# A hybrid retention / differential-attention step: the first attention tiles between the last products of the value projection

## The reference, cut to what matters

```
v_d = h @ w_in[:, 5120:6144]                    # values, 640 tokens x 8 heads of 128
s   = einsum('bqhmd,bkhmd->bhmqk', q, k) * 64**-0.5    # two maps (m = 0, 1) of each head
p   = softmax(s);  a = p[:, :, 0] - lam * p[:, :, 1]
o   = einsum('bhqk,bkhe->bqhe', a, v)
branch_d = (rmsnorm(o) * (1 - lam_init)) @ w_diff_out
```

## Time and profile before

| | |
|---|---|
| median of 3 runs | 1314.18 us (1314.15 to 1314.39) |
| the profiled execution | 1314.83 us, of it the span of the trace 1313.2 us |
| PE busy | 1263.9 us (96%) |
| DVE, ACT, POOL busy | 798.2, 487.5, 307.6 us |
| attention: first scores to last output | 625.25 to 743.6 us |
| a 1 MB weight load | lands a median 5.5 us after its issue |

### The profile page before, as it was taken

The page is one execution under the profiler, slowest core; times in us unless marked ns, Lnnn a source line. Parts: engine busy times, 40 slices in busy tenths (PEclk is TensorE's granted clock), DMA queues, the critical chain, the costliest instruction groups (busy, mean ns, idle before and its releaser), DMA issues.

```text
span 1313.2 us, 19818 instructions
## 1 busy us (share of the span) xinstructions
PE 1263.9 (96%) x7734; PEld 1155.6 (88%) x7734; DVE 798.2 (61%) x1292; ACT 487.5 (37%) x812; POOL 307.6 (23%) x269
## 2 busy tenths in 40 slices
PE   4999999999999999999799899999999999999997
PEld 2698887799999999988688799889998999989986
DVE  4654121466657733463799754378984689547966
ACT  5452223344331112222777532245441244313434
POOL 1011000311000111120699700003520355005500
PEclk9999999999999999999899999999999999999999
DMA  9634222144444434362000034220233122322222
GB/s 307 206 97 136 64 74 71 41 148 141 127 131 130 142 104 127 106 192 97 33 1 1 10 121 153 88 64 27 71 119 106 33 81 89 120 64 64 89 89 80
DMA packets 87392, 129.56 MB, mean 99 GB/s; under 512 B 3529, under 2 KB 64450, under 8 KB 87186
## 3 DMA queue, kind: packets, MB, share of 16 engines
q1 hardware_dynamic: 76880, 95.17, 22.7%
q0 software_dynamic: 9104, 32.20, 8.0%
q10 hardware_dynamic: 1330, 1.10, 0.3%
HBM read 117.43 MB, written 4.73 MB: 93 GB/s over the span
## 4 chain that ended last, share of the span: by engine, by line
PE 85%; POOL 6%; DVE 4%; ACT 3%; issue 1%; DMA 1%; SPq 0%; ACTq 0%; DVEq 0%
PE psum L421 31%; PE psum L458 28%; PE psum L664 17%; POOL probs L961 4%; POOL probs L967 3%; PE psum L1024 1%; PE psum L407 1%; DMA ada_a<-in_w_ada 1%; PE psum L594 1%; PE psum L522 1%; DVE w_lo L390 1%; PE psum L1132 1%; PE psum L1130 1%; PE psum L1131 0%; ACT probs L1531 0%
## 5 line engine op out<-in xcount | busy, mean ns | idle before, releaser
L390 DVE TENSOR_TENSOR w_lo<-w_raw,w_hi 128x2048 fp32r<-128x2048 f32 x57 | 130.6, 2291 | 200.9 <-ACT w_hi L385 197.6
L385 ACT ACTIVATE w_hi<-w_raw 128x2048 fp32r<-128x2048 f32 x57 | 108.8, 1909 | 173.7 <-PE psum L458 107.5
L421 PE MATMUL psum<-h_hi,w_lo 128*128 128x320 f32 x672 | 154.7, 311 | 0.8 <-ACT y_nat L1474 0.8
L421 PE MATMUL psum<-h_hi,w_hi 128*128 128x320 f32 x672 | 153.1, 309 | 0.0
L421 PE MATMUL psum<-h_lo,w_hi 128*128 128x320 f32 x672 | 153.0, 309 | 0.0
L458 PE MATMUL psum<-w_hi,hid 128*128 128x512 f32 x440 | 135.5, 389 | 0.0
L421 PEld LDWEIGHTS psum<-h_hi,w_lo 128*128 128x128 f32 x672 | 111.8, 188 | 1.7 <-issue 1.7
L421 PEld LDWEIGHTS psum<-h_lo,w_hi 128*128 128x128 f32 x672 | 112.3, 188 | 0.0
L421 PEld LDWEIGHTS psum<-h_hi,w_hi 128*128 128x128 f32 x672 | 112.3, 188 | 0.0
L664 PE MATMUL psum<-h_hi,seven_lo 128*128 128x320 f32 x320 | 98.9, 309 | 1.1 <-DVE silu_g L2189 1.1
L664 PE MATMUL psum<-h_lo,seven_hi 128*128 128x320 f32 x320 | 98.9, 309 | 0.0
(11 more groups left out here) (302 smaller groups left out, 2771.7 us busy)
## 6 DMA issues: line engine op xcount, KB each, us to landing
w_raw<-in_w_in SPq DMA_DIRECT2D x32, 1024.0 KB, 5.5
ada_b<-in_w_ada POOLq DMA_DIRECT2D x32, 512.0 KB, 4.0
w_raw<-in_w_ffn_gate SPq DMA_DIRECT2D x11, 1024.0 KB, 5.4
w_raw<-in_w_ffn_up SPq DMA_DIRECT2D x11, 1024.0 KB, 5.4
ada_a<-in_w_ada SPq DMA_DIRECT2D x8, 1024.0 KB, 13.3
w_raw<-in_w_ffn_down SPq DMA_DIRECT2D x8, 1024.0 KB, 5.1
w_raw<-in_w_ret_out SPq DMA_DIRECT2D x4, 1024.0 KB, 5.2
swapped<-qk_d POOLq DMA_DIRECT2D x32, 128.0 KB, 2.6
```

The source lines that it names most:

```text
L385: act.activation(w_hi[s][:, :, :], w_raw[s][:, :, :], ACT.Copy).then_inc(w_hi_done, 1)
L390: dve.tensor_tensor(w_lo[s][:, :, :], w_raw[s][:, :, :], w_hi[s][:, :, :].bitcast(F32), ALU.subtract).then_inc(w_lo_done, 1)
L421: last = pe.matmul(bank(4 * par + 2 * j + h, HALF), w[:, k, cs], x[:, k, h * HALF:(h + 1) * HALF], start=(k == 0 and n == 0), stop=(k == K ...
```

## The change

- The last (i, par) = (1, 1) of `v_d` takes its tiles in the order 0, 2, 1, 3, 4. `scores(0)` stands ahead of it, `scores(1)` behind its third tile, `scores(2)` behind its fourth. The eight matmuls of L407 for both par stand together ahead of `scores(0)`.
- ACT interleaves: both copies of the sums, the table for Exp, `exp(0)`, three tiles of `v_d`, `exp(1)`, a tile, `exp(2)`, a tile. `scores(1)` waits until ACT has copied three tiles of the group.
- The weights of tiles 0 to 2 go to a new buffer `first_probs`, which lies where `w_raw` lies; so SP loads `diff_out`'s weights only after tile 2 has been transposed.
- The split of `diff_out`'s first unit moves into the attention: on ACT four pieces of 128x512 at the end of slots 8 to 11, on DVE eight pieces of 128x256 at the end of slots 14 to 21, each of which reads two tensors of SBUF.
- The prompt keys are transposed (PE) in slot 35 and copied (ACT) there; POOL stores them behind its last tile; DVE waits for that store ahead of `diff_out`'s results. SP stores `new_diff_v`.

The diff, cut to its core:

```diff
+ACT_SPLIT_SLOTS, DVE_SPLIT_SLOTS = range(8, 12), range(14, 22)
...
-        k_out = at("k_out", H + 16, [P, D])
+        k_out = at("k_out", H + 25, [P, D])
         probs = at("probs", H + 20, [P, 3, 2, TOK])
+        first_probs = at("first_probs", W, [P, 3, 2, TOK])
         mix_hi = at("mix_hi", H, [P, KT, TOK], F32R)
...
+        def weights_of(n, m):
+            return (first_probs if n < 3 else probs)[:, n % 3, m, :]
...
+        def act_split_part(act, unit, s, part, parts):
+            ks = slice(part * KT // parts, (part + 1) * KT // parts)
+            if part == 0:
+                act.wait_ge(w_landed[s], (unit - s) * 8 + 16)
+                act.wait_ge(mm_done, unit * 2 - 2 + AHEAD)
+            done = act.activation(w_hi[s][:, ks, :], w_raw[s][:, ks, :], ACT.Copy)
+            if part == parts - 1:
+                done.then_inc(w_hi_done, 1)
+        def dve_split_part(dve, unit, s, part, parts):
+            ks = slice(part * KT // parts, (part + 1) * KT // parts)
+            if part == 0:
+                dve.wait_ge(w_hi_done, unit + 1)
+            done = dve.tensor_tensor(w_lo[s][:, ks, :], w_raw[s][:, ks, :], w_hi[s][:, ks, :].bitcast(F32), ALU.subtract)
+            if part == parts - 1:
+                done.then_inc(w_lo_done, 1)
...
-                        for t in range(TILES):
...
+                            if between and (i, par) == (1, 1):
+                                between(t)
+                    if between and i == 1:
+                        if par == 0:
+                            pe.wait_ge(freed[r], START[name][r] + TILES)
+                            pe.wait_ge(ada_step, 16 * (ADA_FIRST[name] + 3) + 32)
+                            for slot in range(2):
+                                last = sums_over_partitions(pe, slot, bank(1, 4, 4 * slot))
+                            last.then_inc(mm_done, 2)
+                            between(None)
+                        else:
+                            last.then_inc(mm_done, 2)
+                        continue
                     if name in ADA_FIRST:
                         if i == 1 and par == 0:
...
+            sp.dma_start(o["new_diff_v"][0, 0].rearrange("p h e -> p (h e)"), v_d[:, LAT_TILES, :]).then_inc(vd_stored, 16)
+            sp.wait_ge(at_T, 3)
             stream("diff_out", columns(by_tile["w_diff_out"], 0))
             stream_wide("w_o", by_tile["w_o"], 0)
...
-            pool.wait_ge(freed["act"], START["diff_out"]["act"])
-            pool.dma_start(o["new_diff_v"][0, 0].rearrange("p h e -> p (h e)"), v_d[:, LAT_TILES, :]).then_inc(vd_stored, 16)
-            pool.wait_ge(k_copied, 1)
-            pool.dma_start(o["new_diff_k"][0, 0].rearrange("p h m d -> p (h m d)"), k_out[:, :]).then_inc(k_stored, 16)
...
+            pool.wait_ge(k_copied, 1)
...
             pe_dense(pe, "k_d", pe_T_unit, h_hi, h_lo)
-            pe_wide(pe, "v_d", h_hi, h_lo)
-            pe.wait_ge(freed["act"], START["diff_out"]["act"])
             pe.wait_ge(rope_done, 12 + AHEAD)
-            for h in range(DH):
-                last = pe.transpose(bank(6 + h // 4, P, (h % 4) * P), qk_d[:, DH + h, LAT:TOK], ident[:, :])
-            last.then_inc(k_ps, 1)
-            pe.wait_ge(ld_vc, 16)
...
                 b0 = 3 * (n % 2)
                 if n >= 2:
                     pe.wait_ge(at_e, 2 * n - 2)
+                if n == 1:
+                    pe.wait_ge(freed["act"], START["v_d"]["act"] + TILES + 3)
...
             def weights_T(n):
                 full = is_long(n)
+                if n == 0:
+                    pe.wait_ge(freed["act"], START["v_d"]["act"] + TILES + 4)
...
             def outputs(n):
+                if n == 0:
+                    pe.wait_ge(freed["act"], START["diff_out"]["act"])
+                if n == GROUPS:
+                    pe.wait_ge(ld_vc, 16)
                 pe.wait_ge(at_aT, n + 1)
...
-            pe.wait_ge(k_copied, 1)
-            for slot in range(-1, QT + 4):
+            def prompt_keys_T():
+                pe.wait_ge(at_e, 2 * (QT - 1))
+                for h in range(DH):
+                    last = pe.transpose(bank(2 * (h // 4), P, (h % 4) * P), qk_d[:, DH + h, LAT:TOK], ident[:, :])
+                last.then_inc(k_ps, 1)
+            def early_scores(t):
+                if t in (None, 1, 3):
+                    scores((None, 1, 3).index(t))
+            pe_wide(pe, "v_d", h_hi, h_lo, between=early_scores)
+            for slot in range(2, QT + 4):
                 if 0 <= slot - 3 < QT:
                     weights_T(slot - 3)
+                if slot == QT + 1:
+                    prompt_keys_T()
                 if 0 <= slot - 4:
...
                 if slot + 1 < QT:
                     scores(slot + 1)
+            pe.wait_ge(k_copied, 1)
...
             dense("k_d", copy_T("k_d", qk_d, DH, 1.0))
-            dense_wide("v_d", copy_N("v_d", v_d, ACT.Copy, after=12))
-            act.wait_ge(r_ctx_out, RH * 32)
-            act.wait_ge(k_ps, 1)
-            act.activation(k_out[:, :], psum[:, 6 * BANK:8 * BANK], ACT.Copy).then_inc(k_copied, 1)
...
+            def keys_out():
+                act.wait_ge(k_ps, 1)
+                both = psum[:, 0:4 * BANK].rearrange("p (b c) -> p b c", b=2)[:, :, 0:BANK]
+                act.activation(k_out[:, :].rearrange("p (b c) -> p b c", b=2), both, ACT.Copy).then_inc(k_copied, 1)
...
+            act_split(act, unit_of("v_d", 1, 1), 1)
+            act.wait_ge(mm_done, 2 * unit_of("v_d", 1, 0) + 2 + AHEAD)
+            for par in range(2):
+                copy_ada("v_d", 1, par, bank(1, 4, 4 * par)).then_inc(ada_copied, 1)
             set_table(ACT.Exp)
-            for slot in range(QT + 3):
-                if slot >= 3:
-                    evacuate_T(slot - 3)
+            act.wait_ge(w_lo_done, unit_of("v_d", 1, 1) + 1)
+            exp(0)
+            v_d_tiles(1, (0, 2, 1))
+            exp(1)
+            v_d_tiles(1, (3,))
+            exp(2)
+            v_d_tiles(1, (4,))
+            for slot in range(3, QT + 3):
+                evacuate_T(slot - 3)
                 if slot < QT:
                     exp(slot)
+                if slot in ACT_SPLIT_SLOTS:
+                    act_split_part(act, unit_of("diff_out", 0, 0), 0, slot - ACT_SPLIT_SLOTS.start, len(ACT_SPLIT_SLOTS))
                 if slot == QT:
                     set_table(ACT.Sqrt)
+                if slot == QT + 1:
+                    keys_out()
             root("normo", DH * TILES)
             act.wait_ge(gate_T_ps, 1)
...
             dense("k_d", rotate("k_d", qk_d, 8, DH, 4, 128 + 256))
...
             dense_wide("v_d", nothing)
-            dve.wait_ge(freed["act"], START["diff_out"]["act"])
...
+            def late_modulation():
+                dve.wait_ge(ada_copied, 4)
...
+            late_modulation()
...
+                if slot in DVE_SPLIT_SLOTS:
+                    dve_split_part(dve, unit_of("diff_out", 0, 0), 0, slot - DVE_SPLIT_SLOTS.start, len(DVE_SPLIT_SLOTS))
...

```

More of the change, by code:

```diff
@@ L71 @@
 WIDE_BANKS = ((0, 1, 2, 6, 7), (3, 4, 5, 6, 7))
+LAST_TILES = (0, 2, 1, 3, 4)
 def wide_ready(name, i, t):
-    return (2 * WIDE.index(name) + i) * LAT_TILES + t + 1
+    place = LAST_TILES.index(t) if (name, i) == ("v_d", 1) else t
+    return (2 * WIDE.index(name) + i) * LAT_TILES + place + 1
 def lay_out_phases():
@@ L438, in wide, with pe_wide @@
             return w[:, 2 * k:2 * k + 2, :].rearrange("p a b -> p (a b)")
-        def pe_wide(pe, name, hi, lo, kt=KT, split=None):
+        def pe_wide(pe, name, hi, lo, kt=KT, split=None, between=None):
             r, half = READER[name][0], kt // 2
@@ L472, in pe_wide @@
                     else:
-                        for t in range(TILES):
+                        for t in LAST_TILES if between and (i, par) == (1, 1) else range(TILES):
                             if par == 0:
@@ L957, in _ @@
                 first = DVE_KEYS if is_long(n) else 0
-                p0, p1 = probs[:, n % 3, 0, first:size], probs[:, n % 3, 1, first:size]
+                p0, p1 = weights_of(n, 0)[:, first:size], weights_of(n, 1)[:, first:size]
                 pool.wait_ge(at_f, n + 1)
@@ L967, in _ @@
                 pool.tensor_tensor(p0, p0, p1, ALU.add).then_inc(at_a, 1)
+            pool.wait_ge(k_copied, 1)
+            pool.dma_start(o["new_diff_k"][0, 0].rearrange("p h m d -> p (h m d)"), k_out[:, :]).then_inc(k_stored, 16)
             pool.wait_ge(od_rstd, 1)
@@ L1434, in copy_N, with evacuate @@
             def copy_N(name, dst, func, after=0):
-                def evacuate(i):
+                def evacuate(i, tiles=range(TILES)):
                     if after:
                         act.wait_ge(rope_done, after + AHEAD)
-                    for t in range(TILES):
+                    for t in tiles:
                         wait_tile(act, name, i, t)
-                        if name in ADA_FIRST and t == LAT_TILES:
+                        if name in ADA_FIRST and t == LAT_TILES and i == 0:
```

(20 more changed lines are left out.)

14 lines of the change are left out of this document (7 added, 7 removed).

## The result

| | before | after |
|---|---|---|
| median | 1314.29 us (1314.15 to 1315.90, 4 runs) | 1323.62 us (1322.88 to 1324.84, 4 runs) |
| profiled execution, span | 1313.2 us | 1321.2 us |

The ratio is 1.0072, 95% interval 1.0059 to 1.0084: the change makes the kernel 9.3 us **slower**, where 2.1 us faster was forecast, and it lies outside the range of 1307.0 to 1315.0. The cause is one wait of TensorE, 9.1 us long, that the prediction overlooked. It begins some 45 us ahead of the point (606.80) from which the prediction's sum was made.

A forecast was written before the change was run, and what follows sets the result against it. It took four engines within 20% of one attention period, with PE setting the start: -8.0 from the earlier start, +5.8 from DVE's pieces, +0.1 at the end, ACT 0, sum -2.1, median 1312.1 us; range 1307.0 to 1315.0.

The forecast's parts named there:

- The start, by the new order: From the end of `v_d`'s third group (606.80), PE's steps sum to 23.2 us; POOL's first long tile comes 8.0 us earlier.
- Rival 4: Attention's start: POOL's first long tile stays at 638, ACT being the new bound; +5.9, 1320.1 us; chance 0.04.
- the ramp from there to the fifth long tile: Between POOL's first and fifth long tiles: two waits from DVE's evacuation of prompt tiles stay, so the gain remains 8.0 us.
- PE's wait ahead of `scores(1)`: Late in `v_d`, PE waits for ACT's copy of the third tile: 0.23 to start, 0.60 to run, 0.05; 0.88 us.
- ACT's four pieces, slots 8 to 11: In the attention, 0.60 us each in ACT's 0.53 of idle time: taken as 0, at most 0.3 us.
- a piece on DVE: Behind a maximum in slots 14 to 21, it waits for POOL's L967: a slot takes 3.82 us instead of 3.10, +0.72.
- eight pieces: DVE's split in attention slots 14 to 21: eight times +0.72, +5.8 us, with ends of +1.2 and +11.4.
- end of the attention: Eight prompt-key transposes in PE's slot 35, where PE waits for POOL anyway: +0.1 us; stores and weight loads 0.
- Nothing is caught up later: After the slots with DVE's pieces, the time lost stays lost, since PE needs its 3.10 us a slot.
- Rival 1: Slots 14 to 21: pieces slip past POOL and DVE alone pays 1.2 us; -6.7 in all, 1307.5; chance 0.14.
- Rival 2: Slots 14 to 21: a piece begins only behind L967's end plus a hand-over, 0.28 us more a slot; 1314.4; chance 0.14.
- Rival 3: Slots 14 to 21: PE's clock falls because PE idles 0.7 of 3.8 us; +19, 1331 us; chance 0.04.

The follow-up runs named there:

- late_wait: The changed kernel with TensorE's two waits (rope_done, kc_done) moved from ahead of `v_d` into `scores(0)`: 1312.03 us, beside 1314.64 of before.
- wait_only: The kernel before with one line added, TensorE's wait for `rope_done` ahead of `v_d`, and none of the other edits: 1326.40 us, ratio 1.0087.
- four_pieces: late_wait with DVE's low part in four pieces of twice the size, slots 14 to 17, instead of eight: 1310.88 us, ratio 0.9968.
- early_pieces: late_wait with each of DVE's eight pieces ahead of the maximum in its slot instead of behind it: 1307.07 us, ratio 0.9938.

## Why the prediction was wrong, and where it was right

**The step that failed** is the first of "The start, by the new order": "From 606.80". It took the end of `v_d`'s third group as untouched by the change and summed from there. The wait of PE for `rope_done` was in the diff as a line that doesn't move, with `pe_wide("v_d")` going from ahead of it to behind it. The missing term has two parts: 9.1 us of idle PE and 1.5 to 2.2 us of half clock behind it. The traces give 11.40 together for after against late_wait at the end of the third group, and 10.56 there for wait_only against before (+10.4 in the span). That after lies only 10.23 behind before at this point is chance: its trace was 1.26 us ahead when `k_d` ended. The wait needed only rows of before to find, when DVE's last rotation of `k_d` ends against when `v_d` starts:

```profile
563.45 0.39 PE L458 MATMUL psum<-w_lo,h_hi 128*128 128x512 f32 x1
```

```profile
571.44 1.23 DVE L1867 TENSOR_TENSOR qk_d<-rope_tmp,swapped 128x1024 f32 x1
```

The rotation ends at 572.67, 9.2 us behind the start of `v_d`.

Why the step was missed can be read too. I looked for what the change adds at the end of `v_d`, where the scores are, and the search for added waits stopped at the lines with a plus. The wait has none. Rival 4 asked whether the start fails to come earlier, but for a reason in the attention; none of the four rivals stood ahead of `v_d`.

**The other steps**, measured in the trace of after:

| step | forecast | measured |
|---|---|---|
| start, from the third group's end to POOL's first long tile | 23.2, so -8.0 | 23.50, so -7.71 |
| the ramp from there to the fifth long tile | as before, 14.16 | 13.94, so -0.22 |
| start, to the steady part | -8.0 | -7.93 |
| PE's wait ahead of `scores(1)` | 0.88 from the last matmul's step to the scores | 0.84 (0.69 recorded as idle) |
| ACT's four pieces, slots 8 to 11 | 0 | 0 (maxima 3.10, 3.11, 3.10, 3.10 apart) |
| a piece on DVE | 0.72 a slot, slots 3.82 | 0.73, slots 3.83 |
| eight pieces | +5.8 | +5.48 |
| end of the attention | +0.1 | +0.23 |
| TensorE's clock, slots 14 to 21 | 1.00 | 1.00 |

- *The start* came out at -7.93 by two small errors that offset. The two tiles of `v_d` behind scores take 2.94 us each, not 2.75, and the ramp, taken as unchanged, gave 0.22 back.
- *The pieces* were within 0.01 us a slot. The recorded end of the piece is 0.28 behind L1005, not 0.18 as -0.15 + 0.33 gives, but the next reciprocal starts ahead of that recorded end, 0.20 behind L1005 (683.25), and POOL 0.56 behind the reciprocal: the 0.76 are the 0.75 of the sum. "Nothing is caught up later" was not quite right: 0.37 us came back at once (below), which is why eight pieces cost 5.48 and not 5.84.
- *Rival 1* (the pieces slip past POOL) is false for the place behind the maximum and true for the place ahead of it: 0.42 us long, 0.06 a slot.
- *Rival 2* is false: a slot is 3.83, not 4.10. The Trainium skill ("SBUF — State Buffer", section "A bandwidth-pool intuition that's wrong (but worth ruling out)") gives about 115 ns behind the end of VectorE's instruction, measured for GpSimd's descriptors that wait for VectorE. Here it is VectorE that waits for GpSimd, and the trace doesn't bear the figure out for that direction: 0.28 less the 0.27 for the columns leaves about 0.01 us (an estimate from after and four_pieces).
- *Rival 3*: 676 to 708 us has a granted clock of 1.00, with PE idle 3.1 of 32 us there.

With the waits put right the change does what the prediction said: late_wait has 1312.03, the forecast was 1312.1. That the two agree to 0.1 us is in part luck. Beside the before of the same set of runs (1314.64) it is 2.6 us faster, where 2.1 was forecast, and the terms from the third group's end to the scaling of `o_nat` sum to 2.2 (-7.94 + 5.49 + 0.23).

## What to carry to other kernels

When a block of work is moved past a wait, the diff shows the block and not the wait: write down for each engine every wait that now stands ahead of work that it stood behind, with the time at which it is satisfied in the trace of before, and who idles until then. And where two engines are both near a stage's period, ask of an added instruction not only how long it is but what the neighbour runs at the moment it starts: the same low part cost 5.5 us, 0.4 us in another place, or (as two halves, in the drain) nothing. Late_wait with its low part in the drain beats both kernels at 1306.68 us; early_pieces, at 1307.07, can't be told from it (their runs overlap).

## What the runs showed of the hardware that I had not expected

- VectorE's 128x256 subtraction is held up by GpSimd's addition of two tiles (1.09 us) but not by its multiplication by a scalar when it comes 0.86 us into it (0.42 us), although that one reads and writes SBUF as well. The Trainium skill ("SBUF — State Buffer", section "🔬 SBUF: two separate sides") says that a VectorE instruction with two SBUF inputs is blocked by any GpSimd one that reads SBUF; by that the early piece would have waited for L999's end, 0.86 us, and the trace says 0. Whether what the two GpSimd instructions do differently makes this, or how far L999 had got when the piece came, was not tried.
- A one-operand multiplication was held up by the addition as well (0.95 us, ending 0.15 behind it).
- The stage caught up 0.37 us after the last piece: POOL's starts come 3.05, 2.93 and 2.95 apart (706.82, 709.87, 712.80, 715.75), then 3.10 again, with L999 at 1.60 instead of 1.72 in the two tiles between. The prediction had seen the shorter L999 once (652.17 in the earlier trace rows) and gave it no term. The traces show what it goes by: in all 32 long tiles of each of the eight traces L999 (L961 in before) ends 1.43 to 1.44 us behind the end of VectorE's L2055 (L1980 in before), the sum of the two maps for the first keys, which starts ahead of it. Mostly L2055 ends 0.29 us into L999, which then has 1.72; in a backlog it ends some 0.17 into it, and L999 has some 1.60. That fits a GpSimd multiplication which does its work only when VectorE's instruction is done; no run tried it.
- 9.1 us of idle TensorE halved its clock for some 4 us of its next work in after and some 3 us in wait_only (matmuls 0.43 us apart instead of 0.23, 1.2 GHz instead of 2.4), which added 2.21 and 1.49 us to the wait. The idle 3.36 us of before ahead of `scores(2)` had such a stretch too (granted clock 0.81 in 622 to 640); in late_wait the same stretch is at 1.00, and the mean clock of its runs is 0.995 to 0.998 where before has 0.991 to 0.995.
